# Mixer 1's attention with its transposes ahead of the next scores and more turns, its statistics behind the last unit; mixer 2's softmax step in one go around a tap

## The chip, the cores and the metric

One core of one Trainium2 chip runs the whole program. The metric is device time in microseconds (us), the median of three runs: 792.44 us before (791.95 to 795.34).

## What is computed

Two transformer blocks over 256 positions of width 1024, one after the other, all in float32. The parts around the change are the two mixers:

```python
# block 1, mixer 1
proj = rmsnorm(x) @ w_in                      # q,k,v (delta), z, b, a, q_d, k_d, v_d
o_la = gated_delta_rule(q_la, k_la, v_la, g, beta)   # 4 heads, chunks
o_la = rmsnorm(o_la) * silu(z)
# differential attention, 4 heads x 2 query blocks of 128, causal, two maps of 64 each
p = softmax(q k^T + bias);  p = p[map 0] - lam * p[map 1];  o_d = p @ v
o_d = rmsnorm(o_d) * (1 - lam_init)
x = x + concat(o_la, o_d) @ w_out
# block 2, mixer 2
z = h @ w_in_2 + b_in                         # q, k, v, glu_a, glu_b, gate_a, gate_b
a = chunked_rel_attention(q, k, v, rel_bias) @ w_attn_o     # 8 heads
u = silu(layer_norm(causal_dwconv_31(glu_a * sigmoid(glu_b)))) @ w_conv_o
y = (sigmoid(gate_a) * a + sigmoid(gate_b) * u) @ w_mix_o
```

Each block then has a feed-forward network, the second one with a convolution over three positions.

## The kernel before

The weights come as a stream of 512 KB units (`stream()`, line 33), six of them on their way at a time. Most units are split into a high and a low part: ScalarE writes the high one (`whi`), VectorE the low one (`wlo`, raw minus high); this is the step `prep`. TensorE then makes three matmuls per block of 128 rows: L988, L989, L991 in `stat` (a unit is worked off in two half-units of 12 matmuls) and L1027, L1029, L1030 in `movv` and `mov`. Units of kind "a" (`w_ada_2`) are not multiplied on TensorE: VectorE adds each, scaled, to a row sum (`prep`, 1.3 us each). Sixteen of them are woven into mixer 1's units by the condition on line 51.

Nothing is scheduled at run time. `plan()` writes one list of steps, and each engine runs, in this order, those steps that it has a part in. `Plan.fill` takes a PSUM bank for a result, `P.keep(n)` puts in n matmuls of the identity without use, and an engine waits only by semaphores at the instruction that needs the data. So what stands ahead of a step in the list stands ahead of it on every engine of that step.

In mixer 1 (lines 386 to 534) three generators write the list in turns: `main1` (projections: `qk` for the attention's q and k, `movv` for v, units 8 to 11 for the delta rule's v, then z, then w_out), `delta` (the delta rule: `decay`, `em`, `kk`, six levels `lev_y`/`lev_tu`, `vturn`, `solve`, `cross`, `values_la`, `head_la`), and `attention1` (eight units n of one head and one query block). The tuple in `turns(...)` on line 534 says whose turn it is: ten entries, four for main1 and three for each of the others. A unit of `attention1` goes: `scores1` (TensorE: two matmuls; VectorE: bias and maximum; ScalarE: two exponentials with sums), `soft1` (VectorE: reciprocal of the sums; ScalarE: scales map 1), `mix1` (VectorE: combines the maps), `turn1` (TensorE: transposes; ScalarE copies out, to `PT`), `values1` (TensorE: times v; ScalarE copies out, to `odT`). At the end `stats` squares `odT` on VectorE, sums it by matmuls with ones on TensorE (L1255), and takes the power on GpSimd; `head` scales by it and makes mixer 1's second half of w_out's input.

`qk(n)` copies q and k out of PSUM on ScalarE before `scores1` can read them (the wait in `scores`, line 1266). ScalarE's functions need tables; where the next function's table isn't there, an `ACT_TABLE_LOAD` stands ahead of it.

In mixer 2 (lines 625 to 691) `main2`, `conv31` (62 `tap` steps of two VectorE instructions, then `mean`, `variance`, `u2`) and `attention2` (`scores2`, `soft2`, `turn2`, `values2`) take turns evenly. `soft2` is the reciprocal and the scaling of map 0 on VectorE, and the scaling of map 1 on ScalarE; `turn2` waits for both. `gates2` n (tanh on ScalarE) frees the PSUM bank of the gate projections; `four` of `w_attn_o_2` unit u takes bank (0, 1, 6, 7)[u] after it.

## Time and profile before

| | before |
|---|---|
| median of three runs | 792.44 us |
| the profiled execution, its own time | 793.03 us |
| its span, first to last instruction | 791.2 us |
| mean granted TensorE clock | 0.987 of full speed |
| TensorE matmul busy | 755.7 us (96%) |
| VectorE busy | 575.7 us (73%) |
| ScalarE busy | 386.1 us (49%) |
| GpSimd busy | 29.8 us (4%) |
| busy share of the DMA engines by queue 1, the weights | 52.7% |

Mixer 1 lies between about 39 and 209 us of the span, mixer 2 between about 425 and 590 us. A timeline's row gives start, duration, engine, line, operation, output<-input, count, and in brackets the idle time of that engine just before it and what ended it.

### The profile page before, as it was taken

To read this page: it belongs to the slowest core of one execution; us is meant where nothing else is said; L and a number is where in the kernel's file an instruction comes from. 1 tells how busy PE (TensorE), PEld (TensorE's weight loads), DVE (VectorE), ACT (ScalarE), POOL (GpSimd) and SP (SyncE) were. 2 spreads that over 40 slices of the span, in tenths; PEclk is the share of its full clock that TensorE was granted. 3 is DMA by queue.
4 is the path that set the end of the run, shared out by engine and by line. 5 is a ranking of instruction groups with operands and counts; after the bars stand their busy time and mean duration, and the time that the engine had idled before them with its cause. 6 is when DMAs were issued, how large, how long until landed. Compare 5 with 4: busy or idle time off the path is not lost.

```text
span 791.2 us, 13371 instructions
## 1 busy us (share of the span) xinstructions
PE 755.7 (96%) x5302; PEld 695.7 (88%) x5302; DVE 575.7 (73%) x963; ACT 386.1 (49%) x652; POOL 29.8 (4%) x34
## 2 busy tenths in 40 slices
PE   7999999869999999999999999999999999999996
PEld 7978998867899999999979887789979899999995
DVE  5759777657756877678768987687866766766776
ACT  5473234543533453343473443457356555555644
POOL 0030000002000000000013000000000000000000
PEclk9999999978999999999999999999999999999998
DMA  7845243423389988889816623354444655465441
GB/s 289 284 149 182 80 135 105 162 81 127 133 293 402 316 286 275 278 299 326 282 31 214 211 82 107 106 187 157 146 151 149 199 198 200 160 197 202 160 135 53
DMA packets 40526, 148.94 MB, mean 188 GB/s; under 512 B 4496, under 2 KB 4624, under 8 KB 40080
## 3 DMA queue, kind: packets, MB, share of 16 engines
q1 hardware_dynamic: 39600, 142.91, 52.7%
q10 hardware_dynamic: 864, 5.18, 1.7%
q8 instruction: 42, 0.69, 0.3%
q14 instruction: 20, 0.16, 0.1%
HBM read 147.02 MB, written 1.05 MB: 187 GB/s over the span
## 4 chain that ended last, share of the span: by engine, by line
PE 72%; DVE 14%; ACT 8%; issue 4%; DMA 1%; POOL 1%; DVEq 0%; SPq 0%; ACTq 0%
PE bank L988 13%; PE bank L991 13%; PE bank L989 13%; PE bank L1029 6%; PE bank L1027 6%; PE bank L1030 6%; PE bank L1158 4%; DVE arena L1391 4%; DVE wlo L1385 4%; PE bank L1005 3%; PE bank L1018 3%; ACT arena L1921 3%; DVE XN L1391 2%; ACT whi L1921 2%; ACT XN L1921 2%
## 5 line engine op out<-in xcount | busy, mean ns | idle before, releaser
L988 PE MATMUL bank<-hh,whi 128*128 128x256 f32 x1008 | 289.1, 287 | 0.8 <-DVE hl L1385 0.5
L991 PE MATMUL bank<-hh,wlo 128*128 128x256 f32 x1008 | 285.8, 284 | 0.0
L989 PE MATMUL bank<-hl,whi 128*128 128x256 f32 x1008 | 285.7, 283 | 0.0
L1385 DVE TENSOR_TENSOR wlo<-raw,whi 128x1024 fp32r<-128x1024 f32 x202 | 243.3, 1237 | 45.9 <-ACT whi L1921 45.8
L1921 ACT ACTIVATE whi<-raw 128x1024 fp32r<-128x1024 f32 x202 | 202.6, 1047 | 25.6 <-DMA raw<-w_dram 19.6
L988 PEld LDWEIGHTS bank<-hh,whi 128*128 128x128 f32 x1008 | 193.8, 192 | 5.6 <-issue 3.1
L989 PEld LDWEIGHTS bank<-hl,whi 128*128 128x128 f32 x1008 | 193.9, 192 | 1.5
L991 PEld LDWEIGHTS bank<-hh,wlo 128*128 128x128 f32 x1008 | 193.7, 192 | 0.0
L1391 DVE SCALAR_TENSOR_TENSOR arena<-bank,cols,arena 128x255 f32<-128x255 f32 (+3 forms) x138 | 58.9, 480 | 30.4 <-ACT arena L1921 28.8
L1921 ACT ACTIVATE arena<-bank 128x256 f32<-128x256 f32 (+2 forms) x65 | 26.6, 420 | 97.9 <-PE bank L991 71.1
L1029 PE MATMUL bank<-wlo,fh 128*128 128x512 f32 x176 | 69.1, 393 | 1.1 <-DVE wlo L1385 1.1
L1027 PE MATMUL bank<-whi,fh 128*128 128x512 f32 x176 | 69.0, 392 | 0.0
L1030 PE MATMUL bank<-whi,fl 128*128 128x512 f32 x176 | 68.5, 389 | 0.0
L1385 DVE TENSOR_TENSOR arena<-arena,bank 128x512 f32<-128x512 f32 (+1 forms) x57 | 32.1, 582 | 30.3 <-ACT arena L1921 26.1
L1921 ACT ACTIVATE arena<-bank,cols 128x256 f32<-128x256 f32 x60 | 29.2, 534 | 46.5 <-PE bank L991 39.2
L1391 DVE SCALAR_TENSOR_TENSOR XN<-arena,cols,XN 128x256 f32<-128x256 f32 x120 | 49.9, 479 | 0.0
L1391 DVE SCALAR_TENSOR_TENSOR arena<-raw,small,arena 128x1024 f32<-128x1024 f32 x35 | 45.5, 1301 | 1.4 <-DMA raw<-w_dram 1.4
L1158 PE MATMUL bank<-arena 128*128 128x128 f32 x352 | 42.2, 275 | 0.6 <-DVE arena L1385 0.6
L1158 PEld LDWEIGHTS bank<-arena 128*128 128x128 f32 x352 | 40.8, 192 | 0.9 <-DVE arena L1385 0.9
L1921 ACT ACTIVATE arena<-arena 128x256 f32<-128x256 f32 (+2 forms) x37 | 18.7, 510 | 42.9 <-DVE arena L1391 42.7
L1029 PEld LDWEIGHTS bank<-wlo,fh 128*128 128x128 f32 x176 | 33.2, 189 | 7.3 <-DVE wlo L1385 1.8
L1385 DVE TENSOR_TENSOR fl<-arena,fh 128x256 fp32r<-128x256 f32 x48 | 20.4, 425 | 26.1 <-ACT fh L1921 26.1
(168 smaller groups left out, 904.9 us busy)
## 6 DMA issues: line engine op xcount, KB each, us to landing
raw<-w_dram SPq DMA_DIRECT2D x268, 512.0 KB, 4.7
arena<-rows_dram ACTq DMA_DIRECT2D x1, 1792.0 KB, 9.5
X<-x_dram SPq DMA_DIRECT2D x2, 512.0 KB, 4.7
arena<-rows_dram ACTq DMA_DIRECT2D x1, 1024.0 KB, 12.9
arena<-bias_dram ACTq DMA_DIRECT2D x1, 1024.0 KB, 16.2
out_dram<-X SPq DMA_DIRECT2D x4, 256.0 KB, 2.1
const<-const_dram ACTq DMA_DIRECT2D x1, 640.0 KB, 3.9
arena<-bias_dram ACTq DMA_DIRECT2D x1, 512.0 KB, 6.2
```

Of the source, the lines that this page charges most:

```text
L988: e.matmul(o, a, hh[:, k, :], start=(k == 0), stop=False)
L989: e.matmul(o, a, hl[:, k, :], start=False, stop=False)
L991: ins = e.matmul(o, wlo[:, s, k * 128:k * 128 + 128], hh[:, k, :], start=False, stop=(k == 7))
L1005: ins = e.matmul(o, raw[:, i % RAW, k * 128:k * 128 + 128], h32[:, k, :], start=(k == 0), stop=(k == 7))
L1018: ins = e.matmul(o, raw[:, i % RAW, k * 128:k * 128 + 128], h32[:, k, tok(b)], start=(k == 0), stop=(k == 7))
L1027: e.matmul(o, lh[:, k, t0], whi[:, s, c:c + 512], start=first, stop=False)
L1029: e.matmul(o, lh[:, k, t0], wlo[:, s, c:c + 512], start=False, stop=False)
L1030: return e.matmul(o, ll[:, k, t0], whi[:, s, c:c + 512], start=False, stop=last)
L1158: ins = e.matmul(p[:, h, :], lhs(h), rhs(h), start=True, stop=True)
L1385: return e.tensor_tensor(out, a, b, op)
L1391: return e.scalar_tensor_tensor(out=out, in0=a, scalar=s, in1=b, op0=op0, op1=op1)
L1921: return e.activation(out, a, func, scale=scale, **kw)
```

## The change

Nothing is computed in another way; instructions are ordered differently, and one buffer moves.

- Stream: the sixteen "a" units begin after unit 14 instead of unit 10 and are denser (four in five places instead of two in three).
- `attention1`: `turn1` n-1 (and its bank) now stands directly ahead of `scores1` n instead of behind it; `values1` n-1 comes after `soft1` n, and `mix1` n one turn later.
- The turns of mixer 1: eleven entries instead of ten, four for main1, four for attention1, three for delta.
- The squares of `odT` are a step of their own, `squares_od`, for two heads each, behind units 7 and 8; `stats` stands ahead of `head_la`, and `head` only behind it. `sq_od` takes the place of `Ym` (column 2048) instead of that of `qd`, so an assertion asks that the levels are over. The six idle matmuls ahead of the last `turn1` are gone.
- `attention2`: between `scores2` and `soft2` stands a tap (`next(taps, None)`) instead of a turn given back, and unit 7 has no turn more ahead of `turn2`; `conv31` gives back four turns instead of three ahead of `mean`.

```diff
@@ stream
-        if 10 <= n < 34 and n % 3 != 2:
+        if 14 <= n < 34 and n % 5 != 3:
             out.append(early.pop(0))
@@ attention1
         for n in range(9):
+            if n:
+                P.fill(f"pt1{n - 1}")
+                P.step("turn1", n - 1)
+                if n == 8:
+                    flags.add("t7")
             if n < 8:
                 while ("qk", n // 2) not in flags:
                     yield
@@
                 P.step("scores1", n)
             yield
-            if n:
-                P.fill(f"pt1{n - 1}")
-                if n == 8:
-                    P.keep(6)
-                P.step("turn1", n - 1)
-                if n == 8:
-                    flags.add("t7")
             if n < 8:
                 P.step("soft1", n)
-            yield
             while "vd" not in flags:
                 yield
-            if n < 8:
-                P.step("mix1", n)
             if n:
                 h = (n - 1) // 2
@@
                 P.step("values1", n - 1)
                 if n % 2 == 0:
                     P.held.discard(ko)
+            if n < 8:
                 yield
+                P.step("mix1", n)
+                yield
+            if n > 6:
+                assert "lev" in flags
+                P.step("squares_od", n - 7)
+        while "z" not in flags:
+            yield
         P.fill("rs_od")
         P.step("stats")
+        while "la" not in flags:
+            yield
@@
-    turns(main1(), delta(), attention1(), (0, 1, 2, 0, 2, 1, 0, 1, 2, 0))
+    turns(main1(), delta(), attention1(), (0, 2, 1, 0, 2, 1, 0, 2, 1, 0, 2))
@@ conv31
-        for _ in range(3):
+        for _ in range(4):
             yield
         P.fill("mu")
@@ attention2
                 P.step("scores2", n)
-                yield
+                next(taps, None)
                 P.step("soft2", n)
@@
-                if n in (0, 1, 7):
+                if n < 2:
                     yield
                 P.fill(f"pt2{n}", frees=1)
@@ program
-        sq_od = region(4096, 4, T)
+        sq_od = region(2048, 4, T)
@@ VectorE
+            def squares_od(n):
+                for h in range(2 * n + 2):
+                    wait_after(f"pv1{h}1")
+                v, o = odT[:, 2 * n:2 * n + 2, :], sq_od[:, 2 * n:2 * n + 2, :]
+                ts(o, v, 2.0 ** 64, ALU.min, -2.0 ** 64, ALU.max).then_inc(sems["fits"], 1)
+                w.wait_ge("fits", n + 1)
+                stt(o, o, 2.0 ** -16, o, ALU.mult, ALU.mult).then_inc(sems["sqv"], 1)
+
             def stats():
-                for h in range(4):
-                    wait_after(f"pv1{h}1")
-                for n in range(2):
-...
                 sums = wait_full("rs_od")[:, :].rearrange("p (c s) -> p c s", s=64)[:, :, 0]
```

The changed file has seven or eight more lines ahead of these places, so its L995, L1034, L1143, L1280 and L1929 are L988, L1027, L1136, L1273 and L1921 of before.

How the order moves, at three places.

TensorE at the start of mixer 1, before: the last three matmuls of the first q and k units, the first half-unit of v (six matmuls of 512 columns), the sums for the norms of the delta rule (x16), and then the two matmuls of `scores1` 0.

```order
L988 MATMUL bank<-hh,whi 128x256
L989 MATMUL bank<-hl,whi 128x256
L991 MATMUL bank<-hh,wlo 128x256
L1027 MATMUL bank<-whi,hh 128x512
L1029 MATMUL bank<-wlo,hh 128x512
L1030 MATMUL bank<-whi,hl 128x512
L1027 MATMUL bank<-whi,hh 128x512
L1029 MATMUL bank<-wlo,hh 128x512
L1030 MATMUL bank<-whi,hl 128x512
L1136 MATMUL bank<-const,arena 128x128 x16
L1273 MATMUL bank<-arena 128x128 x2
```

The same place in the changed kernel.

```order
L995 MATMUL bank<-hh,whi 128x256
L996 MATMUL bank<-hl,whi 128x256
L998 MATMUL bank<-hh,wlo 128x256
L1280 MATMUL bank<-arena 128x128 x2
L1034 MATMUL bank<-whi,hh 128x512
L1036 MATMUL bank<-wlo,hh 128x512
L1037 MATMUL bank<-whi,hl 128x512
L1034 MATMUL bank<-whi,hh 128x512
L1036 MATMUL bank<-wlo,hh 128x512
L1037 MATMUL bank<-whi,hl 128x512
L1143 MATMUL bank<-const,arena 128x128 x16
```

The scores' two matmuls moved from behind 22 others to directly behind the q and k units that they read.

ScalarE around the silu of units 8 to 11, before: the weights of z 0 (`whi`), the values of unit 3, the copies of the last convolution, the table and the silu, the weights of z 1, the table of the exponential, the exponentials of `scores1` 5, the copy of `turn1` 4, the scaling of `soft1` 5.

```order
L1921 ACTIVATE whi<-raw 128x1024
L1921 ACTIVATE arena<-bank 128x256
L1921 ACTIVATE arena<-bank,cols 128x256 x2
L1921 ACT_TABLE_LOAD
L1921 ACTIVATE arena<-arena 128x1024
L1921 ACTIVATE whi<-raw 128x1024
L1921 ACT_TABLE_LOAD
L1921 ACTIVATE arena,small<-arena,small 128x256 x2
L1921 ACTIVATE arena<-bank 128x128
L1921 ACTIVATE arena<-arena,small 128x256
```

The same place in the changed kernel.

```order
L1929 ACTIVATE whi<-raw 128x1024
L1929 ACTIVATE arena<-bank 128x128
L1929 ACTIVATE arena,small<-arena,small 128x256 x2
L1929 ACTIVATE arena<-bank,cols 128x256 x2
L1929 ACTIVATE arena<-arena,small 128x256
L1929 ACT_TABLE_LOAD
L1929 ACTIVATE arena<-arena 128x1024
L1929 ACTIVATE whi<-raw 128x1024
L1929 ACTIVATE arena<-bank 128x256
```

`turn1` 4 and the exponentials of unit 5 moved ahead of the convolution's copies, the scaling of `soft1` 5 in between these copies and the table load; the last row is the copy of `turn1` 5.

ScalarE at the end of mixer 2, before, from the weights of `w_attn_o_2` 2 on: the last gates (three), the table and the root of `variance`, two weight units, the table and the first silu of `u2`.

```order
L1921 ACTIVATE whi<-raw 128x1024
L1921 ACTIVATE arena<-bank,small 128x256 x2
L1921 ACTIVATE arena<-arena 128x256
L1921 ACT_TABLE_LOAD
L1921 ACTIVATE arena<-arena 128x256
L1921 ACTIVATE whi<-raw 128x1024 x2
L1921 ACT_TABLE_LOAD
L1921 ACTIVATE XN<-XN,cols 128x256
L1921 ACTIVATE ml<-XN 128x256
```

The changed kernel from the table of the root on: the root, the table of gates 6 and these, two weight units, the table and the silus of `u2` (cut), and at the end gates 7.

```order
L1929 ACT_TABLE_LOAD
L1929 ACTIVATE arena<-arena 128x256
L1929 ACT_TABLE_LOAD
L1929 ACTIVATE arena<-bank,small 128x256 x2
L1929 ACTIVATE arena<-arena 128x256
L1929 ACTIVATE whi<-raw 128x1024 x2
L1929 ACT_TABLE_LOAD
L1929 ACTIVATE XN<-XN,cols 128x256
...
L1929 ACTIVATE ml<-XN 128x256
L1929 ACTIVATE arena<-bank,small 128x256 x2
L1929 ACTIVATE arena<-arena 128x256
```

There are three table loads there instead of two, and the gates that free bank 1 moved behind `u2`.

## Rows read from the trace of the kernel before

**Rows 1.** Timeline of TensorE in mixer 1, the rows ahead of which it waited.

```profile
54.18 1.13 PE L1150 MATMUL bank<-arena,const 128*128 128x512 f32 x2 [0.78 <-DVE small L1388]
...
68.32 1.23 PE L1183 MATMUL bank<-const,arena 128*128 128x128 f32 x8 [1.72 <-DVE arena L1385]
...
121.97 3.84 PE L1158 MATMUL bank<-arena 128*128 128x128 f32 x32 [0.62 <-DVE arena L1385]
...
141.37 0.49 PE L1292 MATMUL bank<-arena 128*128 128x128 f32 x2 [3.44 <-ACT arena L1921]
...
168.27 0.41 PE L1281 MATMUL bank<-const,arena 128*128 128x128 f32 x2 [2.02 <-DVE arena L1391]
...
174.47 3.68 PE L1255 MATMUL bank<-const,arena 128*128 128x64 f32 x16 [3.95 <-DVE arena L1391]
```

**Rows 2.** The same view in mixer 2.

```profile
459.10 0.41 PE L1304 MATMUL bank<-const,XN 128*128 128x128 f32 x2 [1.09 <-ACT XN L1921]
...
511.94 0.44 PE L1304 MATMUL bank<-const,XN 128*128 128x128 f32 x2 [1.47 <-ACT arena L1921]
...
523.57 0.63 PE L1304 MATMUL bank<-const,XN 128*128 128x128 f32 x4 [1.75 <-ACT XN L1921]
...
535.89 1.97 PE L1347 MATMUL bank<-XN,const 128*128 128x256 f32 x8 [0.86 <-DVE XN L1391]
```

**Rows 3.** Busy time by stretch: PE, PEld, DVE, ACT, POOL, granted clock, DMA share, GB/s.

```profile
142.00:143.00 1.00, 1.00 (x7) 1.00 (x7) 0.75 (x1) 1.00 (x2) 0.00 (x0) 0.50 0.00 0
145.00:146.00 1.00, 1.00 (x9) 1.00 (x8) 0.13 (x1) 0.84 (x1) 0.00 (x0) 0.79 0.67 250
```

**Rows 4.** Chain of waits: start, us, what; a matmul in that stretch.

```profile
142.49 0.21 PE bank L989
```

**Rows 5.** Timeline of TensorE, end of the first q and k units.

```profile
45.18 0.28 PE L989 MATMUL bank<-hl,whi 128*128 128x256 f32 x1
...
45.30 0.28 PE L991 MATMUL bank<-hh,wlo 128*128 128x256 f32 x1
```

**Rows 6.** Timeline of ScalarE, start of mixer 1.

```profile
49.10 0.64 ACT L1921 ACTIVATE arena<-bank 128x256 f32<-128x256 f32 x2
...
57.90 3.05 ACT L1921 ACTIVATE whi<-raw 128x1024 fp32r<-128x1024 f32 x3
```

**Rows 7.** Timeline of VectorE: em, and the first level's first products.

```profile
60.14 1.89 DVE L1385 TENSOR_TENSOR arena<-arena,small 128x512 f32<-128x512 f32 x3
...
67.49 1.29 DVE L1385 TENSOR_TENSOR arena<-arena,const 128x512 f32<-128x512 f32 x2
```

**Rows 8.** Page, groups of instructions: the row sums of "a" units.

```profile
L1391 DVE SCALAR_TENSOR_TENSOR arena<-raw,small,arena 128x1024 f32<-128x1024 f32 x35 | 45.5, 1301 | 1.4 <-DMA raw<-w_dram 1.4
```

**Rows 9.** Timeline of ScalarE around the silu of units 8 to 11.

```profile
131.80 1.28 ACT L1921 ACT_TABLE_LOAD   x1
...
134.60 1.06 ACT L1921 ACTIVATE arena<-arena 128x1024 f32<-128x1024 f32 x1 [1.52 <-DVE arena L1391]
...
135.57 1.04 ACT L1921 ACTIVATE whi<-raw 128x1024 fp32r<-128x1024 f32 x1
...
140.06 0.51 ACT L1921 ACTIVATE arena<-arena,small 128x256 f32<-128x256 f32 x1 [2.15 <-DVE small L1388]
```

**Rows 10.** Timeline of VectorE in the same stretch.

```profile
131.89 2.68 DVE L1391 SCALAR_TENSOR_TENSOR arena<-bank,cols,arena 128x255 f32<-128x255 f32 x6 [1.88 <-ACT arena L1921]
...
136.65 1.22 DVE L1385 TENSOR_TENSOR wlo<-raw,whi 128x1024 fp32r<-128x1024 f32 x1 [0.88 <-ACT whi L1921]
```

**Rows 11.** Timeline of VectorE at the end of mixer 1.

```profile
154.20 0.69 DVE L1646 TENSOR_REDUCE small<-arena 128x4 f32<-128x512 f32 x1 [0.18 <-ACT arena L1921]
...
156.61 0.69 DVE L1385 TENSOR_TENSOR arena<-bank,small 128x512 f32<-128x512 f32 x1
...
170.60 0.69 DVE L1385 TENSOR_TENSOR ml<-arena,mh 128x512 fp32r<-128x512 f32 x1 [0.69 <-ACT mh L1921]
```

**Rows 12.** Timeline of GpSimd in stats.

```profile
178.50 1.63 POOL L2248 TENSOR_TENSOR small<-small 128x8 f32<-128x8 f32 x1 [12.82 <-DVE small L1388]
```

More of the change, by code:

```diff
@@ L457, in delta @@
                 yield
+        flags.add("lev")
         while "v" not in flags:
@@ L690, in plan @@
     P.step("gate_sums")
-    turns(main2(), conv31(), attention2(), (0, 1, 2))
+    taps = conv31()
+    turns(main2(), taps, attention2(), (0, 1, 2))
     for name, tag in (("w_attn_o_2", "ao"), ("w_conv_o_2", "co")):
@@ L1665, in head_la @@
                 tt(ml[:, 0:4, tok(b)], v, mh[:, 0:4, tok(b)].bitcast(F32), ALU.subtract).then_inc(sems["mixl_la"], 1)
-            def stats():
-                for h in range(4):
-                    wait_after(f"pv1{h}1")
-                for n in range(2):
-                    v, o = odT[:, 2 * n:2 * n + 2, :], sq_od[:, 2 * n:2 * n + 2, :]
-                    ts(o, v, 2.0 ** 64, ALU.min, -2.0 ** 64, ALU.max).then_inc(sems["fits"], 1)
-                    w.wait_ge("fits", n + 1)
-                    stt(o, o, 2.0 ** -16, o, ALU.mult, ALU.mult).then_inc(sems["sqv"], 1)
+            def squares_od(n):
[5 more added lines that the diff above has]
+                stt(o, o, 2.0 ** -16, o, ALU.mult, ALU.mult).then_inc(sems["sqv"], 1)
+            def stats():
                 sums = wait_full("rs_od")[:, :].rearrange("p (c s) -> p c s", s=64)[:, :, 0]
@@ L1891, in _ @@
                 "factors": factors, "em": em, "kk": kk, "kq": kq, "lev_first": lev_first, "lev_y": lev_y, "lev_tu": lev_tu,
-                "vturn": vturn, "cross": cross, "values_la": values_la, "head_la": head_la, "stats": stats, "head": head, "scores1": scores1, "soft1": soft1, "mix1": mix1,
+                "vturn": vturn, "cross": cross, "values_la": values_la, "head_la": head_la, "squares_od": squares_od, "stats": stats, "head": head, "scores1": scores1, "soft1": soft1, "mix1": mix1,
                 "scores2": scores2, "soft2": soft2, "values2": values2, "mod_sum": mod_sum, "gate_sums": gate_sums, "biases2": biases2,
```

## Prediction

> **What bounds the kernel now.** I read the page first: TensorE is busy for 96% of the span, so the time can fall only where TensorE waits or runs at half clock, and it rises by whatever new wait the order brings. Then I read TensorE's timeline and looked for the rows with idle time ahead of them. In mixer 1 there are six [rows 1]: 0.78, 1.72 and 0.62 us in the first 80 us, then 3.44 ahead of `values1` 4, which waits for ScalarE's copy of the transposes, 2.02 ahead of `turn1` 7, and 3.95 ahead of `stats`. In mixer 2 there are four, 5.2 us together [rows 2]. Third, the stretches: after the wait of 3.44 us the granted clock was 0.50, the lower of the two levels (1.2 GHz), and back at 2.4 GHz in the course of the stretch from 145 [rows 3]. A matmul of 256 columns took 0.21 us there [rows 4] and 0.12 elsewhere, as two starts in a row show [rows 5]; so such a spell of 3.5 us costs about 1.8 us beyond the wait. `stats` ran at half clock too (3.68 us).
>
> The last waits of mixer 1 are what the change goes for: 9.4 us in three waits, 1.8 us of low clock behind the first, 1.8 in `stats`, and six idle matmuls of two passes each at 0.12, 1.4 us. All of mixer 1's end could give 14 us at most, mixer 2 5 us.
>
> **Part 1, the start of mixer 1: +6.7 us.** `scores1` 0 now stands directly behind the units whose q and k it reads. Those end at 45.4 [rows 5]. ScalarE's copies of them end at 49.74 [rows 6], because the delta rule's gates and a weight unit stand ahead of them on ScalarE, and nothing the change does moves these. Before, TensorE bridged the time with a half-unit of v and the 16 sums for the norms, which need no such copy. Now it stands still from 45.4 to 49.8: 4.4 us. The wait is longer than the one of 3.44 behind which the clock fell, so I add a spell of low clock, 1.8. The wait of 0.78 in `decay` goes, since the norms' bank is long free: -0.8. Behind `decay` the chain is the same as before: ScalarE's weight units start at 57.90 [rows 6], VectorE runs `em` from 60.14 and reaches the first level's products at 67.49 [rows 7], and TensorE waits for these (the 1.72). VectorE has one row sum of an "a" unit more in this chain, since the first ones come later: +1.3 [rows 8]. Sum 4.4 + 1.8 - 0.8 + 1.3 = 6.7. From below, without low clock and with the 1.72 absorbed: 2. From above 7. I take 6.7, because VectorE ran this chain without a pause, so nothing in it absorbs a delay.
>
> **Part 2, level 5: +1.9 us.** The 0.62 at 121.97 waits for `lev_y` 5 on VectorE. Ahead of it now stand also `scores1` 4 and `soft1` 4 (about 0.8 and 0.3), and the weight unit between them waits on ScalarE behind the exponentials, two of 0.4 to 0.5 each with their sums (0.51 for the larger shape [rows 9]): about 1.0. An "a" unit of 1.3 stands where the first of a sum, without addition, took 0.5 less. That is 2.6, and TensorE arrives 0.5 to 0.7 later with its added steps: +1.9. Bounds 0 and 2.6.
>
> **Part 3, the end of mixer 1: +2.2 us.** The copy of the transposes now goes ahead of the exponentials, so the old 3.44 goes. What is late next is `mix1` 5, for which `turn1` 5 waits. VectorE starts the last convolution at 131.89 and needs 2.68 [rows 10]. Before, ScalarE had its table loaded in that time (131.80) and ran the silu at once at 134.60, then the weights of z 1 [rows 9]. Now the scaling of `soft1` 5 stands ahead of the table load. So behind the convolution come, one after the other: VectorE's reciprocal and product 0.35, the scaling 0.5, the table 1.28, silu 1.0, weights high 1.0, weights low 1.2 [rows 9, 10], `mix1` 0.45: 134.5 + 5.8 = 140.3. TensorE, with one half-unit, the second part of level 6 and another half-unit behind 130.9, is there at 136.0: a wait of about 4.4, with the low clock again. Further on, `scores1` 6 stands directly behind its q and k: 0.75. `solve` 0 waits 0.65 for `vturn`. `turn1` 7 waits about 2.7: ahead of `mix1` 7 VectorE has `values_la` 0, 154.20 to 157.30 with its power on GpSimd inside [rows 11], and the weights behind it. The squares of heads 2 and 3 wait for `values_la` 1 (3.1 again), an "a" unit (1.3) and a weight unit (1.2): TensorE waits 3.1 in the middle of `stats`. And `stats` is now ahead of `head_la` on VectorE, with GpSimd's 1.63 [rows 12]. Then come the first product 0.7, the high half 0.7, the low half 0.7 [rows 11]; TensorE has only `head_la`'s transposes meanwhile and waits 3.3 for w_out's first unit. Together 4.4 + 0.75 + 0.65 + 2.7 + 3.1 + 3.3 = 14.9, against 9.4 + 1.4 (idle matmuls) = 10.8 before; from the 4.1 more goes what `stats` gains if it runs at full clock, 1.8. Rounded: +2.2. From below, if VectorE keeps up and only the wait behind the silu is left: -8. From above, with a second spell of low clock: +5. VectorE's list is in order and its length the nearest rows give, so I stay by the walk.
>
> **Part 4, mixer 2: +0.6 us.** `turn2` 0 stands one half-unit (1.44) earlier while what it waits for comes at the same time: 1.09 + 1.44 = 2.5. `scores2` 1 and 2 stand directly behind their q and k and wait 0.9 each. The 1.47 and the 1.75 [rows 2] go: from unit 2 on ScalarE does the scaling directly behind the exponentials, and there are two whole units of TensorE between scores and transposes. So 4.3 against 4.3. The taps end earlier, as VectorE waited often in this part, and `mean` no longer waits: -0.86. At the end ScalarE has three tables instead of two, and gates 7, which free bank 1 for `w_attn_o_2` 1, stand behind `u2`, 3.9 us of silus and splits. I get the bank free about 1.4 after TensorE asks. Sum +0.6, bounds -3 and +3.
>
> The Trainium skill (ScalarE: Activation LUTs, What ACT_TABLE_LOAD costs) puts a switch at about 1283 ns for the load plus a drain of about 1380 ns, 2.66 us in all. The row shows the 1.28, and none of mine shows a drain, since the silu behind it waited for VectorE anyway. By the page the sum would be 1.4 higher in part 3, where a load is newly on the path, and up to 2.8 in part 4. The sum goes by the row.
>
> **At nothing:** `sq_od` in another place (the levels are over by then), the four turns before `mean`, the "a" units in the DMA queue (the weights' queue is 53% busy, no wait in mixer 1 is a DMA's), `head` behind w_out's second unit (GpSimd's spreads finish under the first). If the low parts of w_out 4 to 7, now behind `head` on VectorE, come late, it costs up to 0.5.
>
> **Sum.** 6.7 + 1.9 + 2.2 + 0.6 = 11.4 us on the profiled execution's own 793.0: 804.4. That execution lies 0.6 above the median of 792.44, so against the median 803.8.
>
> **Rivals.** A measurement of this kernel can tell 0.5%, 4 us, from no change.
> - Faster, 786.5 us. The end of mixer 1 becomes what the order promises: the waits of 3.44 and 3.95 go with both spells of low clock and the idle matmuls, -12.2 in part 3; part 1 costs 6.7, mixer 2 gives 0.5. It decides at the point where `mix1` 5 comes before TensorE has done its two half-units. For it: VectorE is busy only 73%. Against it: its order there, silu and weights ahead of `mix1`.
> - No change, 793 us. The first wait stays 4.4 without the clock falling and is half absorbed, and part 3 gives 3 to 4. For it: behind the wait of 2.02 at 168.27 TensorE still started at full clock. Against it: behind the shorter wait of 3.44 the clock had fallen.
> - Much slower, 809 us. In mixer 2 attention's units lie a quarter closer together, and VectorE needs about 6.2 us per unit where TensorE has 6.9; if each of the last five makes TensorE wait one more microsecond, or ScalarE's three tables hold it longer than their loads, +5. The page named above points this way, through its drain.
>
> **Chances.** Forecast 0.61, faster rival 0.14, no change 0.12, much slower 0.13. So faster 0.14, same 0.12, slower 0.74. The forecast's own range, with the bounds of parts 1 to 4 not all at one end, is 797 to 808; to leave out no more than 2 in 10 it must take in no change and part of the faster case: 787.5 to 809.
>
> **What would show it.** TensorE idle for 4.4 us ahead of the first scores (L1280), and the first level at about 75 instead of 68.3. A wait of over 2 at `lev_tu` 5, one of over 4 at `turn1` 5 released by VectorE, two or three of 3 us around `stats`. In mixer 2 2.5 ahead of `turn2` 0 and 1.4 ahead of `w_attn_o_2` 1. I am wrong if the first scores don't wait, since the copies came earlier, or if `turn1` 5 finds its data.

## The result: 3.4% slower, beyond the forecast range

The changed kernel takes 820.62 us (median of 4 runs, 820.16 to 820.90), the one before 793.73 us beside it (791.95 to 795.34): a ratio of 1.0339, 95% interval 1.0311 to 1.0367. The profiled execution took 820.9 us, with a span of 819.1 (before 791.2).

Of the page of the changed kernel, the busy times:

```profile
PE 766.3 (94%) x5290; PEld 705.2 (86%) x5290; DVE 576.2 (70%) x963; ACT 388.8 (47%) x653; POOL 27.9 (3%) x34
```

TensorE's timeline, changed kernel, the rows with idle time ahead of them that answer to [rows 1] and [rows 2] (start, duration, engine, line, operation, tiles, count, then the idle time and who ended it; the lines stand 7 or 8 lower in the file than before):

```profile
50.54 0.80 PE L1280 MATMUL bank<-arena 64*128 64x128 f32 x4 [4.20 <-ACT arena L1929]
74.66 1.44 PE L1190 MATMUL bank<-const,arena 128*128 128x128 f32 x8 [2.06 <-DVE arena L1392]
108.12 2.05 PE L1165 MATMUL bank<-arena 128*128 128x128 f32 x16 [3.41 <-ACT arena L1929]
135.95 2.07 PE L1165 MATMUL bank<-arena 128*128 128x128 f32 x8 [4.90 <-ACT arena L1929]
159.31 0.66 PE L1288 MATMUL bank<-const,arena 128*128 128x128 f32 x2 [4.72 <-DVE arena L1398]
165.54 0.49 PE L1280 MATMUL bank<-arena 64*128 64x128 f32 x4 [0.75 <-ACT arena L1929]
171.09 1.92 PE L1171 MATMUL bank<-const,arena 128*128 128x128 f32 x8 [2.98 <-ACT arena L1929]
188.24 0.66 PE L1288 MATMUL bank<-const,arena 128*128 128x128 f32 x2 [2.60 <-DVE arena L1398]
199.31 1.97 PE L1262 MATMUL bank<-const,arena 128*128 128x64 f32 x8 [3.14 <-DVE arena L1398]
206.43 0.77 PE L1034 MATMUL bank<-whi,mh 128*128 128x512 f32 x1 [3.44 <-DVE ml L1392]
...
487.54 0.41 PE L1311 MATMUL bank<-const,XN 128*128 128x128 f32 x2 [2.53 <-ACT XN L1929]
574.73 0.39 PE L1102 MATMUL bank<-fh,whi 128*128 128x256 f32 x1 [1.32 <-ACT arena L1929]
```

All of the loss comes in mixer 1. The rows of mixer 1 are, in their order, `scores1` 0, `lev_first`, `lev_y` 3, `lev_y` 5, `turn1` 5, `scores1` 6, `vturn`, `turn1` 7, the middle of `stats`, and w_out's first unit. w_out's first unit starts at 206.43 instead of 178.63, 27.8 us later (0.8 of this is there before any order differs: the last matmul of the first q and k units starts at 46.06 instead of 45.30); `turn2` 0 in mixer 2 starts 28.4 later (487.54 against 459.10 [rows 2]) and the end comes 27.9 later. The waits of mixer 1 add up to 32.2 us, against 12.5 in [rows 1]; and TensorE is busy 10.6 us longer (766.3 against 755.7), though it does six idle matmuls less; with their 1.4 us that is 12.0 us of low clock more. The waits of mixer 2 fall by 1.3 (2.53 and 1.32 against the 5.2 of [rows 2]). 19.7 + 10.6 - 1.3 = 29.0, near the 27.9 (ends of matmuls are modelled).

Where the low clock lies, the stretches of mixer 1 and of mixer 2 show (length, busy times of five engines, granted clock, DMA share, GB/s). First the kernel before:

```profile
40.00:206.00 166.00, 152.68 (x1073) 138.34 (x1072) 119.59 (x221) 68.87 (x129) 14.50 (x10) 0.95 0.40 134
...
425.00:591.00 166.00, 159.94 (x1044) 140.93 (x1042) 131.37 (x279) 80.98 (x159) 8.13 (x6) 1.00 0.43 144
```

Then the changed kernel, the same steps in each:

```profile
40.00:234.00 194.00, 161.49 (x1065) 145.99 (x1064) 119.51 (x221) 69.27 (x129) 12.54 (x10) 0.89 0.36 117
...
453.00:619.00 166.00, 161.39 (x1047) 142.64 (x1046) 132.61 (x281) 83.50 (x161) 8.13 (x6) 0.99 0.43 145
```

TensorE is busy 8.8 us longer in mixer 1 and 1.5 longer in mixer 2. In mixer 2 of this trace the clock fell behind the wait of 2.53, where 1.09 had been before; so what the waits give back there, the clock takes.

Seven of the ten waits stood in the forecast. Three did not: 3.41, 4.90 and 2.98, ahead of `lev_y` 3, `lev_y` 5 and `vturn`, all released by a ScalarE copy into the arena. Neither the delta rule's levels nor the turning of v reads anything ScalarE makes at that time. ScalarE's timeline of the changed kernel ahead of the first of them:

```profile
107.40 0.40 ACT L1929 ACTIVATE arena<-arena,small 128x128 f32<-128x128 f32 x1 [4.65 <-DVE small L1392]
107.71 0.36 ACT L1929 ACTIVATE arena<-bank 128x256 f32<-128x256 f32 x1
```

and VectorE's:

```profile
104.68 1.28 DVE L1398 SCALAR_TENSOR_TENSOR arena<-raw,small,arena 128x1024 f32<-128x1024 f32 x1
105.88 1.22 DVE L1392 TENSOR_TENSOR wlo<-raw,whi 128x1024 fp32r<-128x1024 f32 x1
107.02 0.15 DVE L1718 RECIPROCAL small<-small 128x2 f32<-128x2 f32 x1
```

The copy at 107.71 empties the PSUM bank (a slot that TensorE writes its results to) of `pv1`, the values of a head (`values1` 1). TensorE had filled it by 104.72. The copy stands in ScalarE's list behind `soft1` 2 (the scaling at 107.40), which waits 4.65 us for VectorE's reciprocal, and that stands behind an "a" unit and a weight unit. `lev_y` 3 starts at 108.12, when the copy is done: it was given this bank. The plan deals the banks out in turn, in the order in which steps are written. `take()` passes over a held bank, and `values1` gives up its hold as soon as the step is written. Worked out from both plans: in the changed order the next step on TensorE gets this bank in all three places (Y3 of block 0, Y5 of block 1, vT of block 0); before, after the same three heads, it went to later steps (`lev_tu` 3, `turn1` 4, `scores1` 7). ScalarE's copies at the second and the third place, each ending just ahead of TensorE's start at 135.95 and 171.09:

```profile
135.53 0.36 ACT L1929 ACTIVATE arena<-bank 128x256 f32<-128x256 f32 x1
...
170.58 0.36 ACT L1929 ACTIVATE arena<-bank 128x256 f32<-128x256 f32 x1
```

**Theory B (banks)**: these waits are for the bank. **Rival C (chains)**: ScalarE and VectorE are late with everything, and the bank is only where it shows.

### The profile page after: what moved, and what is told of

Its sections match the earlier page's. It is cut to its first block, busy times and chain, and to the rows that moved or that the text cites. A ratio compares the mean times of both kernels' runs of the same rounds, so it can differ in the third digit from the quotient of the medians.

```text
span 819.1 us, 13345 instructions
## 1 busy us (share of the span) xinstructions
PE 766.3 (94%) x5290; PEld 705.2 (86%) x5290; DVE 576.2 (70%) x963; ACT 388.8 (47%) x653; POOL 27.9 (3%) x34
## 4 chain that ended last, share of the span: by engine, by line
PE 75%; DVE 11%; ACT 8%; issue 4%; POOL 1%; DMA 1%; DVEq 0%; SPq 0%; ACTq 0%; POOLq 0%
PE bank L995 13%; PE bank L996 13%; PE bank L998 13%; PE bank L1036 6%; PE bank L1034 6%; PE bank L1037 6%; PE bank L1012 4%; PE bank L1165 4%; DVE arena L1398 3%; DVE wlo L1392 3%; PE bank L1025 3%; ACT arena L1929 3%; ACT whi L1929 2%; DVE arena L1392 1%; ACT XN L1929 1%
## 5 line engine op out<-in xcount | busy, mean ns | idle before, releaser
L995 PE MATMUL bank<-hh,whi 128*128 128x256 f32 x1008 | 291.6, 289 | 0.7 <-DVE hl L1392 0.5
L1929 ACT ACTIVATE whi<-raw 128x1024 fp32r<-128x1024 f32 x202 | 202.1, 1047 | 26.6 <-DMA raw<-w_dram 18.4
L995 PEld LDWEIGHTS bank<-hh,whi 128*128 128x128 f32 x1008 | 195.8, 194 | 4.7 <-issue 2.3
L1929 ACT ACTIVATE arena<-bank 128x256 f32<-128x256 f32 (+2 forms) x65 | 27.1, 423 | 127.6 <-PE bank L998 68.9
L1034 PE MATMUL bank<-whi,fh 128*128 128x512 f32 x176 | 69.0, 392 | 0.0
L1929 ACT ACTIVATE arena<-bank,cols 128x256 f32<-128x256 f32 x60 | 29.3, 535 | 49.1 <-PE bank L998 40.8
L1165 PE MATMUL bank<-arena 128*128 128x128 f32 x352 | 43.9, 280 | 8.3 <-ACT arena L1929 8.3
L1037 PEld LDWEIGHTS bank<-whi,fl 128*128 128x128 f32 x176 | 33.1, 188 | 7.1
L1929 ACT ACTIVATE arena<-arena 128x256 f32<-128x256 f32 (+2 forms) x37 | 18.7, 509 | 41.9 <-DVE arena L1398 41.1
```

The lines of the kernel that those rows point to most:

```text
L995: e.matmul(o, a, hh[:, k, :], start=(k == 0), stop=False)
L1034: e.matmul(o, lh[:, k, t0], whi[:, s, c:c + 512], start=first, stop=False)
L1037: return e.matmul(o, ll[:, k, t0], whi[:, s, c:c + 512], start=False, stop=last)
L1165: ins = e.matmul(p[:, h, :], lhs(h), rhs(h), start=True, stop=True)
L1929: return e.activation(out, a, func, scale=scale, **kw)
```

## The experiments

**The values' bank held longer.** The hold of `pv1`'s bank ends only when the next head's values are due:

```diff
                 if n % 2:
+                    if n > 1:
+                        P.held.discard(ko)
                     ko = P.take(hold=True)
...
                 P.step("values1", n - 1)
-                if n % 2 == 0:
-                    P.held.discard(ko)
...
+        P.held.discard(ko)
         while "z" not in flags:
```

> The kernel after the change, but the bank of the values of a head (pv1) is handed to nothing else until the next head's values are due; the order of every engine is the same. Theory B (banks): the waits of 3.41 us ahead of lev_y 3, 4.90 ahead of lev_y 5 and 2.98 ahead of vturn, all released by ScalarE's copy of the values of an odd unit, are waits for this one bank. They go to under 1 us each, apart from about 2 us that comes up at lev_tu 5 (VectorE's longer list, as forecast), and with them two or three spells of low clock of 1.8 us: 11.3 - 2 + 3.6 to 5.4 = about 13 us less, so 807 to 809 us and a ratio of 1.018. Rival C (chains): ScalarE and VectorE are late with everything there, and the bank is only where it shows; then the same time is waited one or two steps later (lev_tu 3, lev_tu 5, solve 0, turn1 5) and the kernel stays at 818 to 821 us.

Measured: 807.57 us, ratio 1.0184 (1.0165 to 1.0203), 13.1 us less than the changed kernel. The three waits are gone. TensorE's timeline of this kernel, the rows that take their place or stay:

```profile
131.57 3.84 PE L1166 MATMUL bank<-arena 128*128 128x128 f32 x32 [2.47 <-DVE arena L1393]
150.58 0.66 PE L1289 MATMUL bank<-const,arena 128*128 128x128 f32 x2 [4.72 <-DVE arena L1399]
...
185.44 1.97 PE L1263 MATMUL bank<-const,arena 128*128 128x64 f32 x8 [3.14 <-DVE arena L1399]
192.53 0.76 PE L1035 MATMUL bank<-whi,mh 128*128 128x512 f32 x1 [3.41 <-DVE ml L1393]
```

The 2.47 is the wait at `lev_tu` 5 that was forecast; in the changed kernel the 4.90 just ahead covered it. Theory B holds, rival C falls: the same time did not come back at the next steps.

**The first scores behind the norms again.** A flag, set where `norms` is written, is waited for ahead of the loop over the units:

```diff
+        while "norms" not in flags:
+            yield
         for n in range(9):
```

> The kernel after the change, but the first scores wait in the order until the norms' sums are set, as they did before the change (a half-unit of v and the 16 sums for the norms lie again between the last half-unit of k and scores1 0). Nothing else moves. Both theories: the wait of 4.20 us ahead of scores1 0 goes to under 0.3, the granted clock stays up from 50 to 56 us, and the first level comes at about 69 instead of 74.66: 6 to 6.5 us less, 814 to 815 us. A rival (VectorE's chain em, kk, first level sets this time, and not TensorE's arrival): the first level moves by 2 us at most and the kernel stays at 818 to 820.

Measured: 815.00 us, ratio 1.0283 (1.0255 to 1.0312), 5.6 less than the changed kernel, but its four runs lie at 813 and at 817 (812.77 to 816.80), so the 5.6 is good to about 2 us only. TensorE does not wait for the first scores, and the first level comes at 67.27 instead of 74.66. Of these 7.4 us 1.4 lie ahead of any difference in order (the last matmul of the first q and k units starts at 44.70 against 46.06), which leaves 6.0, as expected.

**Both together.**

> The two edits together on the kernel after the change. Theory B: the gains add up, 13 + 6.3 = 19 us less, 801 to 802 us, a ratio of 1.010; what is left against the kernel before is the wait of 4 to 5 us ahead of turn1 5, 2.6 ahead of turn1 7, and 3 each in the middle of stats and ahead of w_out's first unit, against 9.4 us of waits before. Rival C: only the first 6 us, 814.

Measured: 802.12 us, ratio 1.0116 (1.0096 to 1.0136). 5.5 less than with the bank alone, so the two add up.

**Mixer 2 alone, on the kernel before.**

```diff
-        for _ in range(3):
+        for _ in range(4):
             yield
         P.fill("mu")
...
-                yield
+                next(taps, None)
                 P.step("soft2", n)
...
-                if n in (0, 1, 7):
+                if n < 2:
```

> The kernel before, with mixer 2's part of the change alone (a tap between the scores and the softmax step in place of a turn, four turns ahead of the mean, two turns held back ahead of turn2 0 and 1). The difference of the two traces puts mixer 2 at -0.5 us: turn2 0 was 28.4 us late and the end 27.9. If the parts are independent: 793.2 us, within 0.3% of before, with 2.5 us ahead of turn2 0, 1.3 ahead of w_attn_o_2 1 and no 1.47, 1.75 and 0.86. A rival (mixer 2 was helped by the later start, since queues had run ahead): 796 or more.

Measured: 792.62 us, ratio 0.9996 (0.9982 to 1.0011). Mixer 2's part makes no difference that can be told; the interval reaches from -1.4 to +0.9 us. Its trace has the 2.53 ahead of `turn2` 0 and the 1.32 ahead of `w_attn_o_2` 1, and no wait over 0.3 at `scores2` 1 or 2.

**ScalarE's copy first.** The banks as in the changed kernel, but `soft1` is written behind `values1`. Nothing moves on TensorE and VectorE, since the one has no `soft1` and the other no `values1`:

```diff
-            if n < 8:
+            if n == 0:
                 P.step("soft1", n)
             while "vd" not in flags:
...
                 P.step("values1", n - 1)
...
+            if 0 < n < 8:
+                P.step("soft1", n)
```

> The kernel after the change with its banks as they are, but on ScalarE the copy of a head's values (values1, odd units) stands ahead of the next unit's scaling (soft1) and not behind it; TensorE's and VectorE's order is the same. It splits theory B in its two halves: a bank is only late if what empties it is late. ScalarE is free at 102.8, 133.7 and 168.7 us and waits there for VectorE's soft1, while the values stand ready from 104.7, 130.2 and 168.1. So the three waits shrink by what the scaling held the copy up: 3.41 to about 0.4, 4.90 to 3.4, 2.98 to 1.1. Together 6 us less, 814 to 815 us, a ratio of 1.026, half of what e1_hold_bank gave. If the copy's place does not matter, 820.

Measured: 811.81 us, ratio 1.0235 (1.0219 to 1.0250), 8.8 less than the changed kernel. The three waits in TensorE's timeline:

```profile
104.23 2.05 PE L1167 MATMUL bank<-arena 128*128 128x128 f32 x16 [0.47 <-ACT arena L1931]
130.09 2.08 PE L1167 MATMUL bank<-arena 128*128 128x128 f32 x8 [2.93 <-ACT arena L1931]
164.29 1.07 PE L1173 MATMUL bank<-const,arena 128*128 128x128 f32 x8 [1.03 <-ACT arena L1931]
```

3.41, 4.90 and 2.98 became 0.47, 2.93 and 1.03: 6.9 us. The rest I ascribe to low clock, as TensorE is busy 763.6 us instead of 766.3. The 2.93 that stays is what is still ahead of the copy, two exponentials and a weight unit. So a bank handed on at once costs what its emptying engine has ahead of the copy in its list.

**Idle matmuls in the first wait.** The kernel with the held bank, and `P.keep(15)` ahead of the first scores.

```diff
+                if n == 0:
+                    P.keep(15)
                 for m in range(2):
                     P.fill(f"s1{n}{m}")
```

> The kernel e1_hold_bank, with 15 idle matmuls (two passes each, 3.7 us at the higher level) ahead of scores1 0, inside the wait of 4.22 us; nothing of the work moves. It prices the low clock alone. If the spell behind that wait costs 1.8 us, as in the forecast, and lies on the path: the granted clock stays at 1.00 from 50 to 56 us and the time is 1.8 us less than e1_hold_bank's 807.6: 805.8 us. If VectorE's chain sets the first level anyway, nothing is won (807.6).

Measured: 804.93 us, ratio 1.0146 (1.0129 to 1.0163), 2.6 less than with the bank alone. The stretches around the first scores, first of the kernel with the held bank, then of this one:

```profile
40.00:56.00 16.00, 11.78 (x80) 10.80 (x79) 7.18 (x19) 12.14 (x22) 3.02 (x2) 0.89 0.27 90
```

```profile
40.00:56.00 16.00, 15.13 (x120) 14.24 (x120) 6.43 (x18) 12.30 (x22) 3.61 (x3) 1.00 0.24 74
```

From the first scores to the first level it is 22.07 us instead of 23.66: this spell costs 1.6, near the 1.8 of the forecast.

**`mix1` 5 and 7 directly behind `soft1`.** On the kernel with both edits:

```diff
             if n < 8:
                 P.step("soft1", n)
+            if n in (5, 7):
+                P.step("mix1", n)
...
                 yield
-                P.step("mix1", n)
+                if n not in (5, 7):
+                    P.step("mix1", n)
                 yield
```

> The kernel e3_both, and mix1 5 and mix1 7 stand directly behind soft1 5 and soft1 7, ahead of the weight units between them; all else as in e3_both. Theory V (VectorE's list in order): mix1 5 waited behind the low part of a weight unit that needs ScalarE's silu (142.90 to 144.90 us), though its own input was there at 141.58. The wait of 4.72 us ahead of turn1 5 goes to under 0.5, that of 2.50 ahead of turn1 7 to under 0.6, and one or two spells of low clock with them; about 1 us comes back at scores1 6 or solve 0. Together 8 to 10 us: 792 to 794 us, a ratio of 1.000. Rival S (ScalarE is what is late: scaling, table load, silu, weights): the wait moves to the next unit whose weights come from ScalarE, w_in_z 0 and 1, or to solve 0, and 2 us at most are won: 800.

Measured: 796.15 us, ratio 1.0039 (1.0024 to 1.0054), 6.0 less than with both edits, where 8 to 10 were expected. VectorE's timeline of this kernel:

```profile
141.42 0.48 DVE L1405 SCALAR_TENSOR_TENSOR arena<-arena,small 128x256 f32<-128x256 f32 x1 [0.58 <-ACT arena L1936]
...
144.74 1.22 DVE L1399 TENSOR_TENSOR wlo<-raw,whi 128x1024 fp32r<-128x1024 f32 x1 [2.17 <-ACT whi L1936]
...
152.08 1.23 DVE L1399 TENSOR_TENSOR wlo<-raw,whi 128x1024 fp32r<-128x1024 f32 x1 [0.68 <-ACT whi L1936]
```

`mix1` 5 (141.42) no longer stands behind the weight unit (144.74), and TensorE's timeline shows what comes instead:

```profile
142.05 0.41 PE L1295 MATMUL bank<-const,arena 128*128 128x128 f32 x2 [0.27 <-DVE arena L1405]
...
154.23 2.08 PE L1172 MATMUL bank<-arena 128*128 128x128 f32 x8 [2.84 <-DVE arena L1399]
```

4.72 became 0.27, but `solve` 0 (154.23) now waits 2.84 where it had waited 0.48. Its input, `vturn`'s product, stands on VectorE behind three "a" units, three weight units and two softmax steps. Two of these weight units wait for ScalarE's high parts, 2.17 and 0.68 us, together as long as the new wait. Theory V was right about the two waits. Rival S was right about where the wait goes and, by these two rows, in part about ScalarE; it was wrong about the size (800 us), since 6.0 us were won and not 2. Which of the two engines sets `solve` 0 no run separates.

**Another end of mixer 1.** On top of that:

```diff
+        late = [("prep", i) for i in (42, 43)]
+        for s in late:
+            P.steps.remove(s)
         for b in range(2):
             P.fill(f"oT{b}")
             P.step("head_la", b)
+            if b:
+                P.step("squares_od", 1)
+                P.steps += late
...
-        while "z" not in flags:
+        while "la" not in flags:
             yield
+        yield
         P.fill("rs_od")
         P.step("stats")
-        while "la" not in flags:
-            yield
         yield
         for b in range(2):
-            if b == 0:
-                P.keep(5)
             P.bcast(f"fh_od{b}", b)
```

> The kernel e4_mix_early, with another end of mixer 1: head_la goes straight behind values_la 1 on VectorE, ahead of the units a/4/1 and w_out 2, then the squares of heads 2 and 3; the statistics of the softmax branch come between w_out's second and third unit instead of ahead of the first, and head 0 and 1 one unit later, without the five idle matmuls. Theory V: the 3.14 us in the middle of stats and the 3.41 ahead of w_out's first unit are VectorE's list, and TensorE was held at the lower clock behind them up to 193 us. The first goes, the second becomes about 1.3, low clock gives 2 to 3, the idle matmuls 1.3: about 8 us less than e4_mix_early, 784 to 787 us, a ratio of 0.99. Rival: the squares and head 0 now come too late for w_out's fifth unit, and 2 to 4 us of it are waited there: 788 to 790.

Measured: 792.54 us, ratio 0.9992 (0.9976 to 1.0008), 3.6 less instead of 8. TensorE's waits at the end of mixer 1:

```profile
177.69 0.47 PE L1044 MATMUL bank<-whi,mh 128*128 128x512 f32 x1 [3.38 <-DVE arena L1408]
...
191.09 1.13 PE L1160 MATMUL bank<-arena,const 128*128 128x512 f32 x2 [1.55 <-POOL arena L2266]
```

The wait in `stats` went; the one ahead of w_out's first unit stayed at 3.38 instead of 1.3, and the heads came too soon for GpSimd (1.55, and 0.95 at the second head). VectorE's timeline shows two causes of the 3.38:

```profile
174.57 0.75 DVE L1408 SCALAR_TENSOR_TENSOR arena<-bank,cols,arena 128x512 f32<-128x512 f32 x1 [1.04 <-ACT arena L1939]
176.02 0.69 DVE L1402 TENSOR_TENSOR ml<-arena,mh 128x512 fp32r<-128x512 f32 x1 [0.69 <-ACT mh L1939]
176.63 0.74 DVE L1408 SCALAR_TENSOR_TENSOR arena<-bank,cols,arena 128x512 f32<-128x512 f32 x1
```

`head_la` 0 waits 1.04 for ScalarE's half of z. And the low part that w_out's first unit reads is done at 176.71, but TensorE goes on at 177.69, behind the product of `head_la` 1 (177.37): this unit opens four banks at once, and in this plan the banks of both `head_la` transposes are among them. So TensorE's row names VectorE's product (arena) and not the low part (ml) that it had named before. My own edit had made a wait for a bank, by the rule that the first experiment had just shown.

**The statistics alone.** The changed kernel (mixer 2's part too) with the stream, the turns and attention's order of before, the last without its six idle matmuls; the loop of attention is left out here:

```diff
-        if 14 <= n < 34 and n % 5 != 3:
+        if 10 <= n < 34 and n % 3 != 2:
...
-    turns(main1(), delta(), attention1(), (0, 2, 1, 0, 2, 1, 0, 2, 1, 0, 2))
+    turns(main1(), delta(), attention1(), (0, 1, 2, 0, 2, 1, 0, 1, 2, 0))
```

> The kernel before, with the change's squares (two steps, the first behind turn1 7's mix, without the six idle matmuls) and its waits for the flags, and mixer 2's part; stream, turns and the order of attention as before. The squares of heads 0 and 1 leave the wait ahead of stats: TensorE does half of stats at once and waits for the second half only. The wait ahead of turn1 7 grows from 2.0 to about 3.5, as no idle matmuls stand ahead of it. By the walk w_out starts 1.8 us earlier if the clock does not fall in the longer wait, at the same time if it does: 790.7 to 792.6 us.

Measured: 790.61 us, ratio 0.9965 (0.9953 to 0.9977). This part of the change is a gain of 2 to 3 us, of which the six idle matmuls that are gone can be 1.4. Its two last waits:

```profile
168.57 0.41 PE L1288 MATMUL bank<-const,arena 128*128 128x128 f32 x2 [3.36 <-DVE arena L1398]
174.76 1.97 PE L1262 MATMUL bank<-const,arena 128*128 128x64 f32 x8 [3.62 <-DVE arena L1398]
```

**Two moves only**, on the kernel with the statistics alone: the transposes ahead of the next scores at one unit, and one `mix1` moved.

```diff
+            if n == 5:
+                P.fill(f"pt1{n - 1}")
+                P.step("turn1", n - 1)
             if n < 8:
...
-            if n:
+            if n and n != 5:
                 P.fill(f"pt1{n - 1}")
...
+            if n == 7:
+                P.step("mix1", n)
             yield
```

> The kernel s1_stats_only with two moves of the kind that the change makes everywhere, each at the one place where a wait asks for it: turn1 4 ahead of scores1 5 on every engine (so that ScalarE copies the transposes before it waits for VectorE's scores), and mix1 7 directly behind soft1 7, ahead of values_la 1 and a weight unit on VectorE. Theory V: the 3.44 us ahead of values1 4 and the 3.36 ahead of turn1 7 go, with one spell of low clock; VectorE is then the later engine at vturn, solve 0 and turn1 5 to 7, and gives back 3 to 4 us. Together 3 to 5 us less than s1_stats_only: 786 to 788 us, a ratio of 0.992. Rival: VectorE's list gives all of it back, 790 us, as it did in e4_mix_early, where 2.84 us came up at solve 0.

Measured: 789.62 us, ratio 0.9952 (0.9937 to 0.9967), 1.0 less, hardly more than can be told apart. This falls to the rival in size, 790 us. Both waits went, but others came, ScalarE's (1.73 at 144.04, 1.01 at 150.49) as well as VectorE's (1.09 and 1.04 at the last transposes and the first half of `stats`). The last of them grew, with its half of `stats` still at the lower clock:

```profile
144.04 0.49 PE L1285 MATMUL bank<-arena 64*128 64x128 f32 x4 [1.73 <-ACT arena L1934]
...
173.06 1.97 PE L1267 MATMUL bank<-const,arena 128*128 128x64 f32 x8 [4.06 <-DVE arena L1403]
```

**And the statistics inside w_out.**

```diff
             moving(P.unit("m", "w_out", k), "wo", k, k == 0, False)
+            for b in range(2 * (k == 2)):
+                P.bcast(f"fh_od{b}", b)
+                P.step("head", b)
             yield
...
-        while "z" not in flags:
-            yield
-        P.fill("rs_od")
-        P.step("stats")
+        P.steps.remove(("prep", 43))
+        P.step("prep", 43)
         while "la" not in flags:
             yield
         yield
-        for b in range(2):
-            if b == 0:
-                P.keep(5)
-            P.bcast(f"fh_od{b}", b)
-            P.step("head", b)
+        P.fill("rs_od")
+        P.step("stats")
```

> The kernel f1_two_moves, and stats is done between w_out's first and second unit, head 0 and 1 behind the third, without the five idle matmuls, and the weight unit w_out 2 stands behind the squares. TensorE no longer waits for the squares of heads 2 and 3, 3.62 us in s1_stats_only, and its half of stats runs at the higher clock; it waits instead up to 2 us for the low part of head_la 0. Idle matmuls 1.3, waits 1.5 to 2, clock 1: 4 us less than f1_two_moves, 782 to 784 us, a ratio of 0.987. Rival: head 0 is late for w_out's fifth unit, as VectorE has its weight units in between, and 2 us stay lost: 785 to 786.

Measured: 784.81 us, ratio 0.9891 (0.9876 to 0.9906). That is 4.8 less than with the two moves, and 8.5 less than the kernel before. TensorE's waits at the end of mixer 1, and the whole of mixer 1 as a stretch:

```profile
169.51 0.47 PE L1037 MATMUL bank<-whi,mh 128*128 128x512 f32 x1 [2.21 <-DVE ml L1395]
...
190.47 0.50 PE L1039 MATMUL bank<-wlo,mh 128*128 128x512 f32 x1 [1.54 <-DVE wlo L1395]
```

```profile
40.00:199.00 159.00, 146.23 (x1058) 131.23 (x1057) 120.82 (x223) 68.53 (x129) 14.49 (x10) 1.00 0.43 142
```

The waits at the end are smaller and spread, and the granted clock is 1.00 in all of mixer 1, where it was 0.95 before. TensorE is busy 749.2 us instead of the 755.7 of before: eleven idle matmuls fewer, at two passes of 0.12 each, are 2.6, and 3.9 is the clock; the span is 783.3 against 791.2, so fewer waits are the last 1.4.

## Why the prediction was right in sign and wrong in size

The forecast was 803.8 us, with a range up to 809; measured 820.6. Slower was right, and not by luck alone: with the banks put right the kernel is still at 807.6, and seven of the ten waits stand where they were forecast. Point by point:

- **Part 1.** The wait of 4.4 was 4.20, the first level came at 74.66 (said: about 75). Taken back, the part gives 5.5 to 5.6 us, not 6.7. The clock fell a second time here, behind the 2.06 at the first level, which no part had.
- **Part 2.** The wait at `lev_tu` 5 is 2.47 once the banks are out of the way, 1.85 more than the 0.62 of [rows 1]: the +1.9 of the forecast. In the changed kernel it never appeared, since TensorE stood still just ahead of it.
- **Part 3.** 4.4, 0.75, 2.7, 3.1 and 3.3 were 4.72, 0.75, 2.60, 3.14 and 3.44. The 0.65 at `solve` 0 did not show in the changed kernel and was 0.48 in the kernel with both edits. The kernel of the two `mix1` moves shows that the first and the third were VectorE's list, as the walk had it. The weight unit that stood ahead of `mix1` 5 in that list itself waits for ScalarE (the 2.17 above), which the walk had too. What failed here is the clock: I set `stats` at full clock (-1.8), and its second half ran at the lower level (8 matmuls in 1.97 us, the first half's 8 in 1.00) behind the wait in its own middle. And I had misread the clock of the kernel before, where I said that behind the 2.02 at 168.27 TensorE still started at full clock. The two matmuls of that row did, but the low clock began right behind them and lasted into w_out's first unit, so there was more of it to win or lose than the 1.8 in `stats`:

```profile
168.00:183.00 15.00, 10.29 (x40) 8.93 (x41) 8.06 (x14) 2.86 (x5) 4.22 (x3) 0.54 0.13 41
```

- **Part 4.** +0.6 forecast; alone on the kernel before it measured no difference, with an interval that holds the +0.6 too. 2.53 and 1.32 came as said; the two waits of 0.9 at `scores2` 1 and 2 did not. In its trace, as in the changed kernel's, a spell of low clock behind the 2.53 takes back what the waits give; the forecast did not have it, and the last kernel went through the same 2.53 without one.
- **The drain.** The page named in the prediction (the Trainium skill, ScalarE: Activation LUTs, What ACT_TABLE_LOAD costs) has a drain of about 1380 ns beside the load at every switch to a different set of tables. The changed kernel now shows a load with nothing else to wait for, and no drain beyond the load's 1.28 us. ScalarE's timeline of the changed kernel:

```profile
153.68 0.51 ACT L1929 ACTIVATE arena<-arena,small 128x256 f32<-128x256 f32 x1 [3.08 <-DVE small L1392]
154.21 1.28 ACT L1929 ACT_TABLE_LOAD   x1
155.51 1.06 ACT L1929 ACTIVATE arena<-arena 128x1024 f32<-128x1024 f32 x1
```

- **The step that failed** is the list "At nothing", which stopped at buffers, queues and the "a" units. It left out that a new order of steps deals out other PSUM banks. The walk followed what each step reads and each engine's list; it did not ask, for each fill, who had the bank last and who empties it. That cost 13.1 us of the miss of 16.8. With the bank held, waits of 11.3 us go and the 2.47 at level 5 comes up: 8.8. TensorE is also busy 5.7 us less, which is low clock; the two make 14.5, and the two profiled spans lie 14.1 apart.
- **The rest of the miss**, 807.57 against 803.8, goes with the low clock. With the banks held TensorE is busy 760.6 us, 4.9 more than before, although six idle matmuls of 1.4 us are gone: 6.3 us of low clock more, where the sum had 1.8 - 1.8 = 0. That is 2.5 more than the 3.8 of the miss; I can't give these 2.5 to single terms, though part 1, 1.1 to 1.2 lower than forecast, is the largest that came out lower.

Of the rivals none came true. The faster one needed `mix1` 5 in time, and TensorE waited 4.72 for it. The much slower one came nearest with 809 us, but was still 11.6 short and had the wrong place: mixer 2 gave no loss that can be told.

## What to carry to other kernels

Where banks are dealt out in turn, every reordering also changes who inherits from whom. So list for each fill the last user of its bank and the instruction that empties it, and see where that instruction stands in its engine's list; here a bank held until its next use gave 13 us. Move a step only where a wait asks for it: the same idea (transposes ahead of the next scores, statistics later) lost 27 us when it was made throughout (13 of them through the banks), and was part of a gain of 8.5 (793.3 to 784.8) when it was made at one unit, with one `mix1` and the statistics placed by the waits. Most of the 8.5 came with the statistics: the two moves alone gave 1.0. And a wait that is taken away can return at the next step that hangs on the same lists: 4.72 us gone at `turn1` 5 brought 2.84 at `solve` 0.

## What the runs showed of the hardware that I had not expected

- The length of a wait alone does not decide whether the clock falls. The kernel with the first scores behind the norms and the one with both edits have the same order up to their first level and the same wait ahead of it. Behind it the first ran on at full clock and the second did not (8 matmuls in 1.23 and in 1.71 us):

```profile
67.27 1.23 PE L1193 MATMUL bank<-const,arena 128*128 128x128 f32 x8 [2.30 <-DVE arena L1395]
```

```profile
68.69 1.71 PE L1194 MATMUL bank<-const,arena 128*128 128x128 f32 x8 [2.30 <-DVE arena L1396]
```

- The same holds for the spell of 1.8 us that the forecast took from the wait of 3.44. The kernel with mixer 2's part alone has mixer 1 as before, and the same wait of 3.44 (at 141.94). Behind it the granted clock is 1.00, where it was 0.50 in [rows 3]:

```profile
142.00:146.00 4.00, 4.00 (x34) 3.94 (x34) 3.40 (x5) 3.07 (x5) 0.00 (x0) 1.00 0.39 125
```

- So a single spell of low clock is not a fixed term of a sum, and that one trace has it and another not does not show what an edit did. In the changed kernel even the 3.41 ahead of `lev_y` 3 was followed by 1.00 (108 to 112 us), and the last kernel ran through a wait of 2.21 at 1.00.
- Where the clock is spared at one place it can fall at the next. Behind the 2.47 at level 5 the kernel with the held bank ran at full clock (131.57, 32 matmuls in 3.84 us), the one with the idle matmuls did not:

```profile
127.48 5.47 PE L1168 MATMUL bank<-arena 128*128 128x128 f32 x32 [2.47 <-DVE arena L1395]
```

- Counted from the first scores to that wait, the idle matmuls had won 3.2 us (78.00 against 81.15). By the end of the two profiled executions 0.9 was left (spans 1.8 apart, of which 0.9 lies ahead of the first scores); the medians are 2.6 apart. That the idle matmuls caused the low clock at level 5 is not shown, by the two points above.
